# A two-block transformer on one core: the compression's maps in partition halves, gate logits with weights stationary, compressed values in each quad's bank

## What is computed

```python
q, kc, vc, ks, vs, kw, vw, gl, z = jnp.split(h @ w_in, ...)     # h: 256 x 1024
def compress(t, pos_emb, w1, w2):                               # t: kc or vc, 4 groups, 64 wide
    blocks = t[:, :, cmp_idx] + pos_emb                         # 15 windows of 32 tokens, stride 16
    flat = blocks.reshape(b, g, n_cmp, NSA_CMP_LEN * HEAD_DIM)  # 2048 wide
    return jax.nn.gelu(flat @ w1) @ w2
k_cmp = rms_norm(compress(kc, cmp_pos[0], cmp_w1[0], cmp_w2[0]), k_gain[0])
v_cmp = compress(vc, cmp_pos[1], cmp_w1[1], cmp_w2[1])
pc = masked_softmax(q @ k_cmp * SCALE, cmp_end <= t)            # 16 heads x 256 x 15
o_cmp = pc @ v_cmp
gates = sigmoid(gl)                                             # 256 x 3 x 16 heads
o = gates[0] * o_cmp + gates[1] * o_slc + gates[2] * o_win
return (o * silu(z)) @ w_out
```

## Time and profile before

| | |
|---|---|
| three runs | 906.66, 910.56, 910.5 us; median 910.5 |
| profiled execution | 911.4 us; span of its records 909.6 us |
| granted TensorE clock, mean of the span | 0.966 |
| busy: PE, DVE, ACT, POOL | 838.4, 558.5, 427.4, 119.8 us |
| HBM traffic | 121.5 MB, 133 GB/s over the span |

### The profile page before, as it was taken

How to read it: one execution, slowest core, us unless ns; L and a number is a source line. 1 busy time by engine, 2 the same in 40 slices (tenths; PEclk the granted TensorE clock), 3 DMA queues, 4 the chain that set the end, 5 groups by cost and what they waited for, 6 DMA issues and landing times.

```text
span 909.6 us, 14004 instructions
## 1 busy us (share of the span) xinstructions
PE 838.4 (92%) x5488; PEld 741.4 (82%) x5488; DVE 558.5 (61%) x960; ACT 427.4 (47%) x828; POOL 119.8 (13%) x129
## 2 busy tenths in 40 slices
PE   5999886999968899999889999999999899999997
PEld 4889885777868777899778877887998688999996
DVE  5897474765895746343644645776575665555555
ACT  4434535864453734443644533555343444444443
POOL 1234002531351301000010010011100100000000
PEclk9998998999998999999999999999899999999999
DMA  8645212003533232554231343432455365665551
GB/s 312 179 150 183 93 47 93 2 24 108 186 132 99 87 116 94 184 186 139 93 127 62 96 134 93 126 107 93 162 163 169 132 200 174 205 196 190 174 181 47
DMA packets 93505, 121.50 MB, mean 134 GB/s; under 512 B 8760, under 2 KB 69616, under 8 KB 93440
## 3 DMA queue, kind: packets, MB, share of 16 engines
q1 hardware_dynamic: 92432, 117.80, 40.2%
q0 software_dynamic: 432, 1.57, 0.5%
q10 hardware_dynamic: 576, 1.23, 0.4%
HBM read 119.55 MB, written 1.05 MB: 133 GB/s over the span
## 4 chain that ended last, share of the span: by engine, by line
PE 76%; DVE 13%; ACT 5%; issue 3%; POOL 1%; DMA 1%; POOLq 0%; SPq 0%; DVEq 0%; ACTq 0%
PE bank L400 21%; PE bank L402 20%; PE bank L401 20%; DVE w_lo L1282 3%; ACT w_hi L943 2%; PE bank L528 1%; PE bank L560 1%; ACT tmp L1039 1%; PE bank L542 1%; PE bank L522 1%; DMA raw<-in_a_w_in 1%; DVE small L1371 1%; PE bank L815 1%; PE bank L407 1%; PE bank L406 1%
## 5 line engine op out<-in xcount | busy, mean ns | idle before, releaser
L1282 DVE TENSOR_TENSOR w_lo<-raw,w_hi 128x1024 fp32r<-128x1024 f32 (+1 forms) x217 | 267.5, 1238 | 165.4 <-ACT w_hi L943 163.2
L943 ACT CAST w_hi<-raw 128x1024 fp32r<-128x1024 f32 (+1 forms) x217 | 225.9, 1044 | 178.3 <-PE bank L402 169.7
L400 PE MATMUL bank<-h_hi,w_hi 128*128 128x256 f32 (+1 forms) x800 | 235.1, 294 | 7.7 <-DVE ar L1660 3.7
L401 PE MATMUL bank<-h_lo,w_hi 128*128 128x256 f32 (+1 forms) x800 | 231.4, 289 | 0.0
L402 PE MATMUL bank<-h_hi,w_lo 128*128 128x256 f32 (+1 forms) x800 | 230.6, 288 | 0.0
L400 PEld LDWEIGHTS bank<-h_hi,w_hi 128*128 128x128 f32 x800 | 156.0, 195 | 12.4 <-DVE ar L1660 4.0
L401 PEld LDWEIGHTS bank<-h_lo,w_hi 128*128 128x128 f32 x800 | 156.1, 195 | 0.3
L402 PEld LDWEIGHTS bank<-h_hi,w_lo 128*128 128x128 f32 x800 | 156.3, 195 | 0.0
L400 PE MATMUL bank<-w_hi,h_hi 128*128 128x512 f32 (+2 forms) x304 | 121.1, 398 | 8.8 <-DVE h_lo L1289 5.0
L402 PE MATMUL bank<-w_hi,h_lo 128*128 128x512 f32 (+2 forms) x304 | 118.8, 391 | 0.0
L401 PE MATMUL bank<-w_lo,h_hi 128*128 128x512 f32 (+2 forms) x304 | 118.5, 390 | 0.0
(11 more groups left out here) (306 smaller groups left out, 1248.1 us busy)
## 6 DMA issues: line engine op xcount, KB each, us to landing
raw<-in_w_in SPq DMA_DIRECT2D x24, 1024.0 KB, 5.1
raw<-in_a_w_in SPq DMA_DIRECT2D x14, 1024.0 KB, 5.7
raw<-in_w_ffn_gate SPq DMA_DIRECT2D x11, 1024.0 KB, 5.4
raw<-in_w_ffn_up SPq DMA_DIRECT2D x11, 1024.0 KB, 5.3
raw<-in_w_ffn_down SPq DMA_DIRECT2D x11, 1024.0 KB, 5.1
raw<-in_b_w_in SPq DMA_DIRECT2D x9, 1024.0 KB, 5.4
raw<-in_w_gate SPq DMA_DIRECT2D x8, 1024.0 KB, 5.3
raw<-in_a_w_out SPq DMA_DIRECT2D x4, 1024.0 KB, 5.1
```

The source lines that it names most:

```text
L400: mm(o, lh, rh, start=start, stop=False)
L401: mm(o, lh, rl, start=False, stop=False)
L943: nc.scalar.copy(split(w_hi, s), rawsub(s)[0]).then_inc(S["hi_ready"], 1)
L1282: V.tensor_tensor(split(w_lo, s), rawsub(s)[0], split(w_hi, s).bitcast(F), ALU.subtract).then_inc(S["lo_ready"], 1)
```

## The change

The position bias is no longer computed by itself. kT gets a fifth group of 256 columns, kT_pos, zeroed by POOL at the start, into which DVE copies the positions from gcol; the compression's matmuls read five groups (75 columns), and column 0 of the fifth is the bias. The compression runs over l outside and k (keys, values) inside, and k = 1 goes to partitions 64 to 127, so that GELU runs once on 128 partitions with 60 columns; w2 and vrep lie accordingly. The gate logits are computed with weights stationary: w_hi's slot of a_gl holds the upper and the lower part side by side (96 columns), 16 matmuls stream 256 tokens each, ACT copies the 96 x 256 result to gl_raw, two transposes behind z tile 0 turn it round, DVE adds the two parts, ACT takes the tanh. The tables for heads are made for one item first and for the four others after the fourth rope item, each in three operations. The scores L664 go to banks 4 and 5; behind them attention(0) starts at once, with z tiles 6 and 7 and the transposes of pc within its first two jobs. The eight matmuls with the compressed values are spread: two at the start of each quad, straight into the quad's bank, to which pv adds; the copies to og and the add in take go.

```diff
-        kT = [ar[:, 8192 + 1024 * i:9216 + 1024 * i].rearrange("p (g n) -> p g n", g=4) for i in range(2)]
+        kT = [ar[:, 8192 + 1280 * i:9472 + 1280 * i].rearrange("p (g n) -> p g n", g=5) for i in range(2)]
+        kT_pos = ar[:, 8192:10752].rearrange("p (k n) -> p k n", k=2)[:, :, 1024:1280]
...
-        posb = sm[0:64, 538:540]
-        hidT = sm[0:64, 540:668].rearrange("p (k g c) -> p k g c", k=2, g=4)
+        posb = sm[:, 538:539]
+        hidT = sm[:, 540:604].rearrange("p (g c) -> p g c", g=4)
...
+        cmx_ps = ps[2][:, 64:144].rearrange("p (g c) -> p g c", g=5)[:, :, 0:CMP]
+        xh = tmp[:, 0:64].rearrange("p (g c) -> p g c", g=4)[:, :, 0:CMP]
+        vrep = tmp[64:P, 256:512].rearrange("p (g r c) -> p g r c", g=4, r=4)
+        gl_raw = ar[0:96, 11264:11264 + T]
...
+            if s == first["a_gl"]:
+                lo = 0 if ring is w_hi else 48
+                return w_hi[:, s % RING, 0:2 * a * b].rearrange("p (a b) -> p a b", a=a)[:, :, lo:lo + b]
...
-                        pe.wait_ge(S["cm_oacc"], 4)
+                        pe.wait_ge(S["cm_ptsb"], 1)
...
+                def compressed_weights():
+                    pe.wait_ge(S["cm_p"], 1)
+                    for j in range(4):
+                        last = nc.tensor.transpose(ps[4][:, P * j:P * j + P], pc[:, P * j:P * j + P], ident)
+                    last.then_inc(S["cm_pt"], 1)
+
+                def compressed_values(quad):
+                    pw = pcT.rearrange("p (t h n) -> p t h n", t=2, h=2)
+                    for f in (2 * quad, 2 * quad + 1):
+                        half = f // 4
+                        mm(ps[6 + quad % 2][:, T * (f % 2):T * (f % 2) + T], vblk[half][:, P * (f % 4):P * (f % 4) + P], pw[:, :, half, :],
+                           start=f % 2 == 0, stop=True, skip_group_check=f % 2 == 1)
...
+                    if phase == 0 and j % JQ[phase] == 0:
+                        compressed_values(quad)
...
-                                              start=br == 0 and kt == 0, stop=br == (1 - phase) and kt == qt)
+                                              start=bool(phase) and kt == 0, stop=br == (1 - phase) and kt == qt, skip_group_check=not phase)
...
+                    if phase == 0 and j < 2:
+                        z_tiles(phase, z0, 6 + j, 7 + j)
+                        if j == 1:
+                            compressed_weights()
...
-            pe.wait_ge(S["ld_w1"], 32)
-            for k in range(2):
-                for l in range(16):
-                    last = mm(ps[7][0:64, k:k + 1], w1[:, k, l, :], gcol[:, 24 + 16 * k + l:25 + 16 * k + l], start=(l == 0), stop=(l == 15))
-            last.then_inc(S["cm_bias"], 1)
...
-            tm_panel(first["a_gl"], hx(h_hi), hx(h_lo), (2, 3), width=48, rows=8)
+            s = first["a_gl"]
+            weights_ready(s)
+            both = w_hi[:, s % RING, 0:96 * KT].rearrange("p (a b) -> p a b", a=KT)
+            for kt in range(KT):
+                last = kt == KT - 1
+                if last:
+                    mm(ps[2][0:48, 0:T], both[:, kt, 0:48], tok(1, kt), start=False, stop=False, skip_group_check=True)
+                o = mm(ps[2][0:96, 0:T], both[:, kt, :], tok(0, kt), start=kt == 0, stop=last)
+                if not last:
+                    mm(ps[2][0:48, 0:T], both[:, kt, 0:48], tok(1, kt), start=False, stop=False, skip_group_check=True)
+            o.then_inc(S["sub_used"], 1)
             za = first["a_z"]
-            z_tiles(0, za, 0, 2)
+            z_tiles(0, za, 0, 1)
+            pe.wait_ge(S["gl_raw"], 1)
+            for tt in range(2):
+                o = nc.tensor.transpose(ps[3][:, 96 * tt:96 * tt + 96], gl_raw[:, P * tt:P * tt + P], ident[0:96, 0:96])
+            o.then_inc(S["gl_ps"], 1)
+            z_tiles(0, za, 1, 2)
...
+            pe.wait_ge(S["cm_posw"], 1)
+            cm_out = [cmx_ps[64 * k:64 * k + 64] for k in range(2)]
+            for l in range(16):
+                for k in range(2):
+                    last = mm(cm_out[k], w1[:, k, l, :], kT[k][:, :, 2 * l:2 * l + 16 * (CMP - 1) + 1:16], start=l == 0, stop=l == 15)
...
-                    last = mm(ps[2 + qt][:, 32 * h:32 * h + 32], q_st[:, h // 2, h % 2, P * qt:P * qt + P],
+                    last = mm(ps[4 + qt][:, 32 * h:32 * h + 32], q_st[:, h // 2, h % 2, P * qt:P * qt + P],
                               kc[:, h // 4].rearrange("p i c -> p (i c)"), start=True, stop=True)
             last.then_inc(S["cm_s"], 1)
-            z_tiles(0, za, 6, 8)
-            pe.wait_ge(S["cm_p"], 1)
-            for j in range(4):
-                last = nc.tensor.transpose(ps[3][:, P * j:P * j + P], pc[:, P * j:P * j + P], ident)
-            last.then_inc(S["cm_pt"], 1)
-            pe.wait_ge(S["cm_ptsb"], 1)
-            pe.wait_ge(S["tq_dve"], 8)
-            for f in range(8):
-                half = f // 4
-                o = mm(ps[4 + f // 2][:, T * (f % 2):T * (f % 2) + T], vblk[half][:, P * (f % 4):P * (f % 4) + P],
-                       pcT.rearrange("p (t h n) -> p t h n", t=2, h=2)[:, :, half, :], start=True, stop=True)
-                if f % 2:
-                    o.then_inc(S["cm_o"], 1)
...
+                    if phase == 0 and 1 <= j <= 2:
+                        z_tanh(phase, z0, 5 + j)
...
-            for tt in range(2):
-                A(gate[:, tt].rearrange("p b h -> p (b h)"), ps[2 + tt][:, 0:48], ACT.Tanh, scale=0.5).then_inc(S["gl_t"], 1)
+            nc.scalar.copy(gl_raw, ps[2][0:96, 0:T]).then_inc(S["gl_raw"], 1)
             za = first["a_z"]
+            split_hi_to(za + 5)
+            z_tanh(0, za, 0)
+            act.wait_ge(S["gl_x"], 1)
+            A(sm[:, 48:144], sm[:, 48:144], ACT.Tanh, scale=0.5).then_inc(S["gl_t"], 1)
...
-                    if phase == 0:
-                        dve.wait_ge(S["cm_oacc"], 4)
-                        link(V.tensor_tensor(g, o, g, ALU.add))
-                        V.tensor_tensor(g, g, zs[:, 2 * q:2 * q + 2, :], ALU.mult).then_inc(S["og_ready"], 1)
-                    else:
-                        V.tensor_tensor(g, o, zs[:, 2 * q:2 * q + 2, :], ALU.mult).then_inc(S["og_ready"], 1)
+                    V.tensor_tensor(g, o, zs[:, 2 * q:2 * q + 2, :], ALU.mult).then_inc(S["og_ready"], 1)
...
+                        z_gate(phase, 5 + j)
+                        if j == 2:
+                            dve.wait_ge(S["cm_pt"], 1)
+                            V.tensor_copy(pcT, ps[4][:, :]).then_inc(S["cm_ptsb"], 1)
...
+            V.tensor_copy(kT_pos[:, :, 0:32:2], gcol[:, 24:56].rearrange("p (k l) -> p k l", k=2)).then_inc(S["cm_posw"], 1)
...
+            def head_tables(i, n):
+
+                t, g = tabs[:, i:i + n], gb[:, i:i + n, :]
+                link(V.tensor_tensor(t[:, :, 0], bc(tabs[:, 1, 0], [P, n, 2, HD], 1), bc(g, [P, n, 2, HD], 2), ALU.mult))
+                for a, b in ((0, 32), (32, 0)):
+                    link(V.tensor_tensor(t[:, :, 1, :, a:a + 32], bc(tabs[:, 1, 1, :, a:a + 32], [P, n, 2, 32], 1),
+                                         bc(g[:, :, b:b + 32], [P, n, 2, 32], 2), ALU.mult))
+
+            head_tables(0, 1)
...
+            head_tables(2, 4)
...
+            V.tensor_copy(glo, glv[:, :, 0]).then_inc(S["gl_x0"], 1)
+            dve.wait_ge(S["gl_x0"], 1)
+            V.tensor_tensor(glo, glo, glv[:, :, 1], ALU.add).then_inc(S["gl_x"], 1)
...
+            link(V.tensor_copy(posb, cmx_ps[:, 4, 0:1]))
+            link(V.tensor_scalar(xh, cmx_ps[:, 0:4], posb, None, ALU.add))
...
+            V.scalar_tensor_tensor(out=hidT[:, :, 0:CMP], in0=xg, scalar=1.0, in1=xh, op0=ALU.add, op1=ALU.mult).then_inc(S["cm_hid"], 1)
```

77 lines of the change are left out of this document (26 added, 51 removed).

## The result

The changed kernel takes 900.1 us (median of four runs, 898.9 to 900.8), the one before it 910.5 us (906.7 to 912.5, four runs beside it). The ratio is 0.9895, 95% interval 0.9866 to 0.9924: faster, by 10.4 us where 17.1 were forecast. 893.4 us was predicted with a range of 888.5 to 900.0, so the measured time lies 0.1 us above the top of the range, and the forecast was wrong: right in direction, 6.7 us too low.

The account below looks back on a forecast made before the run. TensorE, busy 92% of the span, was taken to bound the kernel. Gains of 12.4 + 2.3 + 1.75 + 0.65 = 17.1 us, and 0.9 for the median, take 911.4 to 893.4 us; range 888.5 to 900.

Parts of the forecast that it names:

- Step 1: Position bias: removing its matmuls and the half clock behind saves 7.0 us, less w_lo waits; gate panel 6.0 us earlier.
- Rival (a): DVE and ACT keep more: w_lo waits of 4 us in all, detour 1.3 us later; 897.7 us, chance 0.17.
- Step 2: Gate logits: 16 matmuls in 1.9 us, z tiles at full clock; compression starts at 90.4 instead of 102.82.
- rival (e): Gate panel: 48- and 96-column matmuls also pull the clock down, costing 2 us; 895.4 us, chance 0.07.
- The detour: Gate logits' way through DVE and ACT, then kT copies and last transposes; compression forecast 16.5 us after the panel's start.
- Step 3: Compression in alternating halves: 74 ns a record (57 to 113), 4.7 us in all, 2.1 us won.
- rival (b): Compression: the halves don't overlap, 113 ns a record, 7.2 us; 895.9 us, chance 0.10.
- Step 4: Attention start: sixth job's scores at S + 20.05 (S: end of L664), net 1.75 us won, plus 0.65 at DVE's take.
- the upper end (+3.3): Attention start: net gain if the half-clock stretch there also goes, instead of the 1.75 us taken.
- Rival (c): Attention start: the overlap buys nothing, -2.8 us instead of +1.75; 898.0 us, chance 0.13.
- Everything behind 200 us should only be shifted: Code after 200 us: keeps its duration; a differing time there would mean the account of the gain is wrong.
- Rival (d): Before the compression: clock falls to half until attention starts, 17 us won, 23 lost; 916 us, chance 0.03.

Follow-up runs that it names:

- pool_eighth: Changed kernel with GpSimd scaling one head instead of eight in the first four rope items, the rest left unnormalised: 893.2 us in one run.
- multiply_deferred: Changed kernel with GpSimd's four query multiplies done only after the second a_c item, nothing left out: 894.5 us, ratio 0.9822 to the kernel before.
- bias_back: Changed kernel with the 32 one-column bias matmuls put back ahead of the a_c panel, into a bank nobody reads: 901.4 us.
- gate_sum_first: Changed kernel with DVE adding the transposed gate logits ahead of the two w_lo that stood before them: 895.9 us, ratio 0.9844 to the kernel before.
- gates_back: Changed kernel with the gate logits computed as before the change (tokens stationary, 48 columns streamed): 902.4 us.
- halves_apart: Changed kernel with all compression records of the first partition half ahead of all of the second, not in turn: 903.4 us in one run.
- before_deferred: Kernel before the change with only GpSimd's four query multiplies moved behind the second a_c item: 909.8 us, ratio 0.9998 to the kernel before.
- attention_back: Changed kernel with the start of the attention as before the change, its copies and additions included: 902.2 us.

## Why the prediction was wrong

**Step 1 failed, with the term for w_lo.** I costed a w_lo at 1.15 us each, from a place where GpSimd was idle, and laid 6 x 1.15 end to end; in the forecast the waits came out at 0.35 + 0.6 us. In the query panels the w_lo come in pairs behind a rope item, and each pair takes 3.21 us. The evidence was in the timeline of DVE of the kernel before, in the very stretch that I was costing, and I did not read it:
```profile
50.78 3.21 DVE L1282 TENSOR_TENSOR w_lo<-raw,w_hi 128x1024 fp32r<-128x1024 f32 x2
```
Three pairs at 0.85 and the tables, 2.3 us and not 1.6, are 3.3 us more; DVE began the first pair 0.4 us earlier than I had laid out (35.42 against 35.8), which leaves 2.9, and the tables do end at 56.05 and not at 53.2. Against the forecast 0.95, the waits were 3.7 us (2.7 more), and 1.6 us of half clock came behind the longest: together 4.3 of the missing 4.6, and for 0.3 I have no row. pool_eighth and multiply_deferred, which take away the overlap and with it the stall and its half clock, give back 4.5 and 5.0.

Behind that size stands a wrong picture. I took the bias matmuls as 7.0 us that TensorE gets back, less two small waits. bias_back shows that they can stand there again for 0.2 us, as long as the half clock behind them takes the place of that behind the stall: DVE had no gap from 30 to 65 us, so once TensorE had overtaken it, what TensorE saved became waiting. Rival (a) named this, and its sign ("waits of TensorE for w_lo above 1 us") was the right one; but I gave it 4 us in all and no clock behind it.

**Step 2, half right.** Sixteen matmuls in 1.9 us at full clock and z tiles at full clock, as forecast; rival (e) fell. The detour ended at +17.8 instead of +16.5. For 0.8 us of it the pair of w_lo in front of the sum took 3.20 us for the same reason as in step 1; the other 0.5 lie between the copies and the compression, where the last transposes ran at half clock (0.50 from 94 to 96 us). I had named the chain sum, tanh, copies but not asked whether it had to stand behind that pair; gate_sum_first shows 2.7 us there. Of the gain against before, 1.6 us were the length of a half-clock stretch that does not always last so long (gates_back).

**Step 3, right in the number taken, by analogy.** 64 records in 4.54 us, 71 ns each, against 74 and 4.7. halves_apart confirms that the turns do it, and rival (b) fell. The halves run fully side by side, which I had only as the lower end, at 57 ns; that end was too low since a record takes 129 ns and not 113. The price of a column in it was wrong as well: the 79 ns of a one-column record mix 58 ns at full clock with 107 at half clock (58 throughout in before_deferred). The Trainium skill, "TensorE: Matmul & The Clock Gate", Part 3, says that a load overlaps matmuls in flight only with another row group; both halves use all 128 rows, and 71 against 125 ns says that it overlaps here all the same.

**Step 4, too low.** S + 20.6 for the sixth job against S + 20.05, 1.03 us for each later pair of value matmuls against 0.93. Yet the time from the scores' end to the projection fell from 68.5 to 63.7 us: 4.8 us were won where 1.75 + 0.65 = 2.4 were counted (attention_back: 4.3, in which its own value matmuls lost 1.7 to half clock). The surplus lies behind the sixth job: 43.1 us to the projection instead of the 46.0 that the forecast amounts to. Before, the first 4 us there ran at 0.51; after, at 1.00, which is 2.0 us, and TensorE waits 0.9 us in that stretch instead of 2.0. I had kept the clock as the upper end (+3.3); the stretch stood in the earlier trace rows. The half clock has come ahead of the sixth job instead, and is in the S + 20.6. That step 4 gave more than counted is luck as much as the clock is. Rival (c) fell.

**"Everything behind 200 us should only be shifted"** was wrong by 2.6 us in this execution, and by between 3.0 us less and 2.9 more time than before in those of the other kernels with the change. Rival (d) foresaw a clock that falls once, ahead of the compression (it did, 0.63 over 9 us, at no cost to the compression itself), but not that the later stretches fall differently in each execution.

The sum: 17.1, less 4.6 at the panel, less 1.3 in the detour, less 0.2 in step 3, plus 2.4 in step 4, less 2.6 behind, is 10.8, as the span gained. The first two terms have causes that runs show; the last two are in large part where the half clock fell in the two profiled executions.

## What to carry to other kernels

When an engine that another one feeds is made faster, the first question is how far ahead the feeder is and what it costs per unit in exactly that stretch, with whatever runs beside it; a lead that was built up in a pause goes with the pause. Elementwise work on GpSimd is not free beside DVE operations that read two tensors from SBUF: put it where DVE has gaps. And a gain of a few us in a kernel whose clock falls in short stretches cannot be read off one profiled execution of each side: here the same code differed by up to 3 us between executions of one program, and the gate panel's start by 1.6 between two kernels in neither of which TensorE waited in front of it.

## What was unexpected about the hardware

A w_lo (128x1024, both inputs in SBUF) takes 1.23 us alone and a GpSimd multiply of 128x512 takes 1.04; started some 0.1 us apart, the pair of w_lo takes 3.21 instead of 2.36 (one of the two lasts 2.07) and the multiply 2.02. That reads like taking turns whole: the multiply waits for the first w_lo, the second w_lo for the multiply. The Trainium skill, "SBUF — State Buffer", in "SBUF: two separate sides", calls the port pair of these two engines an exclusive lock that the loser waits for in full, and counts DVE operations with two SBUF inputs among its users; the trace agrees. The rope products, whose first input is in a bank, show no stretch: in multiply_deferred they run beside the four deferred multiplies and take what they take elsewhere (0.42, 0.28 and 0.28 us, with GpSimd idle, at 58.93). DVE, then POOL:
```profile
64.62 0.41 DVE L1334 TENSOR_TENSOR tmp<-bank,ar 128x256 f32<-128x256 f32 x1
64.95 0.27 DVE L1335 TENSOR_TENSOR tmp<-bank,ar 128x128 f32<-128x128 f32 x1
65.15 0.28 DVE L1336 TENSOR_TENSOR tmp<-bank,ar 128x128 f32<-128x128 f32 x1
```
```profile
60.70 6.43 POOL L1940 TENSOR_TENSOR ar<-ar,small 128x512 f32<-128x512 f32 x4 [9.98 <-DVE ar L1343]
```

A stall of 2.4 to 2.7 us of an otherwise busy TensorE was followed by 3 to 4 us of half clock in six of eight executions, and by none in the two others, though seven of the eight ran the same code up to there. Twenty matmuls whose result nobody reads, put into the stall, kept the clock at 1.00 in both executions.

A matmul of one column followed the last after 58 ns at full clock and 107 at half clock (before), so its pace goes with the clock; the compression's records of 75 columns into one half kept 129 ns at both.
